# A decoder layer with a mixture of experts: the sample tile in quarters, the first rows block by block, states and most bias rows loaded later

## What is computed

```python
sh1, sc1, g1, sh2, sc2, g2 = split(silu(c) @ w_ada + b_ada, 6)   # per sequence
h = rmsnorm(x, norm1) * (1 + sc1) + sh1
u, gate_b, gate_c, val = split(h @ w_in)                         # 4 x 512 columns
pool_out = (window_mean(u, prefix=state_pool) - u) @ w_pool * pool_scale
conv_out = gate_b * depthwise_conv3(gate_c * val, prefix=state_conv)
x = x + g1 * (concat(pool_out, conv_out) @ w_out)
h2 = rmsnorm(x, norm2) * (1 + sc2) + sh2
logits = h2 @ w_router + b_router                                # top 4 of 32, softmax
y = sum over the 4 of gate * expert(h2)                          # clamped SwiGLU, three 1024x1024
out = rmsnorm(x + g2 * y, final_norm)
```

## Time and profile before

| what | us |
|---|---|
| median of three runs | 1306.57 (1305.33 to 1307.25) |
| the profiled execution's own time | 1306.41 |
| its span, first to last instruction | 1304.6 |
| TensorE busy | 1255.8 (96%) |
| VectorE busy | 525.5 (40%) |
| GpSimd busy | 230.4 (18%) |
| ScalarE busy | 90.9 (7%) |

### The profile page before, as it was taken

The page is one execution under the profiler, slowest core; times in us unless marked ns, Lnnn a source line. Parts: engine busy times, 40 slices in busy tenths (PEclk is TensorE's granted clock), DMA queues, the critical chain, the costliest instruction groups (busy, mean ns, idle before and its releaser), DMA issues.

```text
span 1304.6 us, 32026 instructions
## 1 busy us (share of the span) xinstructions
PE 1255.8 (96%) x14083; PEld 578.7 (44%) x14083; DVE 525.5 (40%) x823; ACT 90.9 (7%) x166; POOL 230.4 (18%) x296
## 2 busy tenths in 40 slices
PE   3999999869999999999999999999999999999997
PEld 2687764523444444333333333333444444433344
DVE  1222313556444444444333333333444444444356
ACT  3210011210000000000000000000000000000002
POOL 5001200030111111122222211121111111112100
PEclk9899999969999999999999999999999999999999
DMA  9877762268999999999999999999999999999994
GB/s 323 278 278 279 274 261 94 104 260 347 408 424 424 426 426 425 425 426 420 421 427 424 423 429 416 425 426 424 425 423 417 427 428 424 427 427 425 423 422 156
DMA packets 63430, 487.32 MB, mean 374 GB/s; under 512 B 11191, under 2 KB 20759, under 8 KB 38053
## 3 DMA queue, kind: packets, MB, share of 16 engines
q1 hardware_dynamic: 47442, 455.92, 84.3%
q0 software_dynamic: 10592, 19.87, 4.2%
q10 hardware_dynamic: 5363, 11.05, 2.3%
HBM read 468.22 MB, written 25.88 MB: 379 GB/s over the span
## 4 chain that ended last, share of the span: by engine, by line
PE 93%; DVE 3%; DMA 2%; issue 1%; ACT 1%; SPq 0%; POOL 0%; DVEq 0%; POOLq 0%
PE acc L1943 51%; PE acc L1968 24%; PE acc L943 9%; PE acc L987 4%; DMA raw<-in_w_ada 2%; PE acc L860 1%; PE acc L2050 1%; PE acc L878 1%; PE acc L998 1%; ACT h_t L486 0%; PE acc L2066 0%; DVE picked L1624 0%; PE acc L959 0%; PE acc L983 0%; POOL rows L1412 0%
## 5 line engine op out<-in xcount | busy, mean ns | idle before, releaser
L1943 PE MATMUL acc<-raw_b,ht 128*32 128x512 f32 x3024 | 332.9, 596 | 5.7 <-DVE ht L1578 5.7
L1943 PE MATMUL acc<-raw,ht 128*32 128x512 f32 x2928 | 319.8, 592 | 0.0
L1681 DVE TENSOR_TENSOR g_sb<-acc,bias_gu 128x768 f32<-128x768 f32 x32 | 30.7, 958 | 521.9 <-PE acc L1943 521.9
L1412 POOL DMA_INDIRECT rows<-h_rows,row_next x90 | 92.7, 1030 | 701.3 <-DVE row_next L1573 654.1
L1943 PEld LDWEIGHTS acc<-raw_b,ht 128*32 128x32 f32 x3024 | 98.3, 111 | 234.7 <-issue 228.2
L1943 PEld LDWEIGHTS acc<-raw,ht 128*32 128x32 f32 x2928 | 95.1, 110 | 205.7 <-issue 200.4
L1968 PE MATMUL acc<-raw,at 128*32 128x256 f32 x2976 | 166.3, 379 | 0.0
L1968 PE MATMUL acc<-raw_b,at 128*32 128x256 f32 x2976 | 166.3, 379 | 0.0
L1968 PEld LDWEIGHTS acc<-raw_b,at 128*32 128x32 f32 x2976 | 96.7, 110 | 77.1 <-issue 18.5
L1968 PEld LDWEIGHTS acc<-raw,at 128*32 128x32 f32 x2976 | 96.7, 110 | 63.9
L943 PE MATMUL acc<-h_t,raw 128*128 128x288 f32 (+1 forms) x512 | 120.1, 397 | 1.1 <-DVE h_t L700 1.1
(11 more groups left out here) (257 smaller groups left out, 646.4 us busy)
## 6 DMA issues: line engine op xcount, KB each, us to landing
raw<-in_w_down SPq DMA_DIRECT2D x33, 2048.0 KB, 12.0
raw<-in_w_gate SPq DMA_DIRECT2D x31, 2048.0 KB, 9.1
raw<-in_w_up SPq DMA_DIRECT2D x31, 2048.0 KB, 13.4
raw_b<-in_w_gate SPq DMA_DIRECT2D x31, 2048.0 KB, 9.8
raw_b<-in_w_up SPq DMA_DIRECT2D x31, 2048.0 KB
raw_b<-in_w_down SPq DMA_DIRECT2D x31, 2048.0 KB
raw<-in_w_ada SPq DMA_DIRECT2D x24, 1024.0 KB, 11.7
expert_rows<-zeros ACTq DMA_DIRECT2D x1, 8704.0 KB, 30.6
```

Source lines behind the costliest of these rows:

```text
L1412: pool.indirect_dma_start(rows[:, b, :], None, h2_quarter, bass.IndirectOffsetOnAxis(ap=idx[:, b:b + 1], axis=0), bounds_check=Q * NTOK - ...
L1681: dve.tensor_tensor(g_sb[:, :, :], gate_of(i, 0), plus(0), ALU.add).then_inc(g_read, 1)
L1943: mm = pe.matmul(gu_of(i)[b][q * TB:(q + 1) * TB, :].rearrange("p (m n) -> p m n", m=2), ht_of(i)[:, b, k, :], w[:, kk, :, q * CW:(q + 1) ...
```

## The change

Five things are edited.

1. **Loads.** Of the bias rows only SH1 and SC1 are loaded at the start (`ada_bias`); G1 to G2, the parameters and the states are issued on ScalarE's queue after its half of the modulation, and four loads of the sample rows in quarters (`x_q`) follow. G1's addition waits for the later biases.
2. **State transposes** move from ahead of SH1's last chunk to between project(2) and project(3); their copies on ScalarE (`empty_states`) stand behind leave(3), ahead of the issue of the clearing transfer and leave(4).
3. **Sample tile.** It is added, scaled and shifted as 128 partitions x 256 columns (`x_q`, `h_q`, `g1_q`, `a2_q`). Its sum of squares is joined over the quarters by a product with `same_s`, made by GpSimd. Its rows are stored in four transfers issued by ScalarE; GpSimd spreads each part's sample rows in four transfers instead of one. ScalarE copies the rows back into `x_sb` for the end.
4. **New states.** "so0" goes from ahead of mix(4) to behind transposes h3; the sample's from behind router(3) to behind the routing matmuls.
5. **First expert.** The three gathers count on semaphores of their own; VectorE turns each block when it has landed, and TensorE does the first half of the contraction block by block (`gate_up_first`), then the second half as before. The sums of the gates on VectorE move behind these transposes.

```diff
@@ ScalarE, front
-            for q in range(Q):
-                lo_, hi_ = q * CPAD, q * CPAD + NC
-                act.dma_start(mod[lo_:hi_, :].rearrange("p (a n) -> p a n", n=QW),
...
+            def ada_bias(a, b, loaded):
...
+            ada_bias(SH1, SC1 + 1, rows_loaded)
             act.wait_ge(tp_full, TP["c"] + 1)
             act.activation(c_sg[:, :, :], c_ps, ACT.Sigmoid).then_inc(tp_free, 1)
             norm_row(n1_rows, norm1, rows_loaded)
-            act.dma_start(par_rows[0:GR, :], pool_scale[0].rearrange("(g p) -> g p", p=P)).then_inc(state_loaded, 16)
-            act.dma_start(par_rows[GR:4 * GR, :], w_conv[0].rearrange("w (g p) -> (w g) p", p=P)).then_inc(state_loaded, 16)
-            act.dma_start(sp_rows, state_pool[0].rearrange("b r d -> (b r) d")).then_inc(state_loaded, 16)
-            act.dma_start(sc_rows, state_conv[0].rearrange("b r d -> (b r) d")).then_inc(state_loaded, 16)
...
                                bias=cols[:, 1, k % 2, k // 2, 0:1]).then_inc(h_mod_a, 1)
+            act.dma_start(par_rows[0:GR, :], pool_scale[0].rearrange("(g p) -> g p", p=P)).then_inc(state_loaded, 16)
+            act.dma_start(par_rows[GR:4 * GR, :], w_conv[0].rearrange("w (g p) -> (w g) p", p=P)).then_inc(state_loaded, 16)
+            act.dma_start(sp_rows, state_pool[0].rearrange("b r d -> (b r) d")).then_inc(state_loaded, 16)
+            act.dma_start(sc_rows, state_conv[0].rearrange("b r d -> (b r) d")).then_inc(state_loaded, 16)
+            ada_bias(G1, PARTS, n2_loaded)
+            for q in range(Q):
+                act.dma_start(x_q[q * NS:(q + 1) * NS, :],
+                              x_sample.rearrange("b t d -> (b t) d")[:, q * QW:(q + 1) * QW]).then_inc(xq_loaded, 16)
...
             for g in range(GR):
                 leave(g, uext[:, g, PAST:PAST + SEQ], uext_s[:, g, :, PAST:PAST + DEC_T])
+                if g == GR - 1:
+                    empty_states()
@@ ScalarE, tail
+            act.wait_ge(x1_ready, TT)
+            act.activation(junk[:, 0:QW], x_q[:, :], ACT.Square, accum_out=ss_q[:, 0:1]).then_inc(act_step, 1)
+            turned(f"h{PT - 1}", PT - 1)
+            act.wait_ge(ss_summed, 1)
+            act.activation(rstd_q[:, :], ss_ps, ACT.Sqrt, bias=eps_c[:, 0:1], scale=1.0 / D).then_inc(sq_done, 1)
+            store(PT - 1)
+            empty(f"h{PT}", h_t[:, :, SEQ:NTOK].rearrange("p (q h) s -> p h q s", q=Q),
+                  tp[:, 0, 0:QW].rearrange("p (h q s) -> p h q s", h=KT // Q, q=Q))
+            act.wait_ge(h_ready, TT + PT + 1)
+            for q in range(Q):
+                act.dma_start(h2_dram[SEQ:NTOK, q * QW:(q + 1) * QW], h_q[q * NS:(q + 1) * NS, :])\
+                    .then_inc(h2_stored[PT % 2], 16)
@@ VectorE, tail
+            dve.wait_ge(mix_done, TT)
+            dve.wait_ge(xq_loaded, 16 * Q)
+            step(dve.tensor_tensor(h_q[:, :], mixp[PT % 2][:, 0, 0:QW], g1_q[:, :], ALU.mult))
+            dve.tensor_tensor(x_q[:, :], x_q[:, :], h_q[:, :], ALU.add).then_inc(x1_ready, 1)
+            dve.wait_ge(x1_ready, TT)
+            step(dve.tensor_tensor(h_q[:, :], x_q[:, :], a2_q[0][:, :], ALU.mult))
+            best(PT - 2)
+            dve.wait_ge(sq_done, TT + 1)
@@ TensorE
-            for k in range(4):
+            for k in range(3):
                 project(k)
+            pe.wait_ge(state_loaded, 16 * 4)
+            take("par")
...
+            project(3)
@@ TensorE, tail
+            pe.matmul(ss_ps, same_s[:, :], ss_q[:, 0:1], start=True, stop=True).then_inc(ss_summed, 1)
+            router(3)
+            take("h4")
+            pe.wait_ge(h_ready, TT + PT + 1)
+            for half in range(KT // Q):
+                mm = pe.transpose(tp[:, 0, half * P:(half + 1) * P], h_q[:, half * P:(half + 1) * P], ident[:, :])
@@ VectorE, first expert
+                def turn_first():
+                    for b in range(SB):
+                        dve.wait_ge(first_gathered[b], 16)
+                        ins = dve.transpose(ht[:, b, :, :], rows[:, b, :].rearrange("p (i k) -> p k i", k=KT))
+                        ins.then_inc(first_turned, 1)
@@ TensorE, first expert
+                def gate_up_first():
...
+                    for b in range(SB):
+                        pe.wait_ge(first_turned, b + 1)
+                        for k in range(KT // 2):
...
+                    mm.then_inc(mm_done, MCH)
+                    gate_up(0, MCH // 2)
...
+                pe.wait_ge(so_ready, 4)
```

More of the change, by code:

```diff
@@ L402, in _ @@
                                         pattern=[[-1, DEC_B], [0, DEC_T]], channel_multiplier=1))
+            step(pool.memset(same_s[:, :], 0.0))
+            for m in range(Q):
+                v = same_s[:, :].rearrange("p (q s) -> p q s", q=Q)
+                step(pool.affine_select(out=v, in_=v, compare_op=ALU.not_equal, fill=1.0, base=-NS * m,
+                                        pattern=[[0, Q], [-1, NS]], channel_multiplier=1))
             step(pool.memset(sel_4[:, :], 1.0))
@@ L621, in _ @@
                     act.wait_ge(rstd_ready, 1)
-                act.activation(ss[0:r, t:t + 1], ss[0:r, t:t + 1], ACT.Sqrt, bias=eps_c[0:r, 0:1],
+                act.activation(ss[:, t:t + 1], ss[:, t:t + 1], ACT.Sqrt, bias=eps_c[:, 0:1],
                                scale=1.0 / D).then_inc(sq_done, 1)
[L624 to L640, removed]
+                if t < PT - 1:
+                    turned(f"h{t}", t)
@@ new lines, in _ @@
+            act.wait_ge(h_ready, TT + PT + 1)
+            for q in range(Q):
+                act.dma_start(h2_dram[SEQ:NTOK, q * QW:(q + 1) * QW], h_q[q * NS:(q + 1) * NS, :])\
+                    .then_inc(h2_stored[PT % 2], 16)
+            act.wait_ge(so0_full, 1)
+            states(0, acc_u)
+            for q in range(Q):
+                act.activation(x_sb[0:NS, PT, q * QW:(q + 1) * QW], x_q[q * NS:(q + 1) * NS, :], ACT.Copy)\
+                    .then_inc(xs_rows, 1)
+            act.wait_ge(so_full, 1)
@@ L642, in _ @@
+            states(2, tp)
+            act.wait_ge(so_ready, 4)
+            for i in range(DEC_T):
+                act.dma_start(new_pool_sample[0, :, PAST - DEC_T + i, :], gate_b[i:NS:DEC_T, 2, 0:DP])\
+                    .then_inc(state_sent, 16)
+            act.dma_start(new_conv_sample[0].rearrange("b r d -> (b r) d"), state_o[3]).then_inc(state_sent, 16)
         @block.vector
@@ L945, in project @@
                     mm.then_inc(z_done, 1)
-            for k in range(4):
+            for k in range(3):
                 project(k)
+            pe.wait_ge(state_loaded, 16 * 4)
+            take("par")
+            pe.transpose(tp[:, 0, 0:4 * GR], par_rows[:, :], ident[0:4 * GR, 0:4 * GR]).then_inc(tp_full, 1)
+            take("st")
+            for g in range(GR):
+                n = DEC_B * PAST
+                pe.transpose(tp[:, 0, g * n:(g + 1) * n], sp_rows[:, g * P:(g + 1) * P], ident[0:n, 0:n])
+            for g in range(GR):
+                n = DEC_B * CPAST
+                mm = pe.transpose(tp[:, 1, g * n:(g + 1) * n], sc_rows[:, g * P:(g + 1) * P], ident[0:n, 0:n])
+            mm.then_inc(tp_full, 1)
+            project(3)
             ada(G1)
@@ L1053, in _ @@
             mm.then_inc(rank_done, 1)
+            pe.wait_ge(new_packed, 4)
+            for g in range(GR):
+                pe.transpose(tp[0:NS, 0, g * P:(g + 1) * P], u_new[:, g, :], ident[:, :])
+            for g in range(GR):
+                mm = pe.transpose(tp[0:DEC_B * CPAST, 1, g * P:(g + 1) * P], v_new[:, g, :], ident[:, :])
+            mm.then_inc(so_full, 1)
         part.close()
@@ L1162, in hybrid_step @@
             row_gathered = sem("row_gathered")
+            first_gathered = [sem(f"first_gathered{b}") for b in range(SB)]
+            first_turned = sem("first_turned")
             g2_spread = sem("g2_spread")
```

169 lines of the change are left out of this document (84 added, 85 removed).

## The result

| | before | after |
|---|---|---|
| median of the runs, us | 1306.86 | 1311.51 |
| lowest and highest, us | 1304.03 to 1307.34 | 1309.99 to 1313.42 |
| profiled execution: time, span, us | 1306.41, 1304.6 | 1309.99, 1308.2 |

The change made the kernel slower: the ratio of the times is 1.0041, with a 95% interval of 1.0028 to 1.0054. That is 5.3 us above the forecast and half a microsecond above its range. The profiled execution of the changed kernel was the shortest of its six, so of these 5.3 us only the 4.0 between the forecast difference of -0.4 and the measured one of +3.6 can be followed in a trace. Medians here are over all executions; two of e2's (1449 and 1858 us) and one of e6's (2253 us) were far longer than the rest, and the ratios leave them out.

The account below looks back on a forecast made before the run. TensorE was taken to bound the kernel from 305.09 us to the end, so only earlier stretches could move: -6.2 (c) + 0.4 (a and b1) + 3.7 (b2) + 1.7 (b3) = -0.4, giving 1306.2 us, range 1304.0 to 1309.0.

Parts of the forecast that it names:

- (b3): Projection: TensorE's clock falls once more than before behind the longer waits, a loss of 1.7 us.
- (b1): Projection's third slice: twelve DMAs queued ahead of leave(0) delay it 5.75 us; less slack 2.2 and front gain 3.1, +0.4.
- (b2): Between project(2) and project(3): the moved state transposes and ScalarE's copies make TensorE wait, a loss of 3.7 us.
- (c): From router(2) to the first expert: earlier ids, quartered sample tile and block-wise start gain 6.2 us.
- (a): Ahead of the projection: transposes leave the chain and fewer loads compete, a gain of 3.1 us (1.7 to 3.6).
- Rival 2: Projection: ScalarE's queue becomes the bound, issues take 9 us, both waits let the clock fall; 1311.2 us, chance 0.17.
- The early slow stretch: Start of the projection: clock at 0.50 from 39 to 45 us; no gain if it goes.
- rival 1: Tail: stores land within 4.8 us, ids release the gathers, at most one clock fall; 1302.0 or 1303.7 us, chance 0.31.
- Rival 3: First expert: block 0 comes no earlier than the others, only the path ahead of the gathers gains; 1309.8 us, chance 0.10.

Follow-up runs that it names:

- e2: The changed kernel with its front put back as before, the x_q loads staying on ScalarE's queue: 1302.28 us, ratio 0.9963 to before.
- e6: Changed kernel, twelve DMAs behind leave(1), parameter and state copies behind leave(4), SyncE's weight loads of slots 4 and 5 held until rows are stored: 1299.14 us.
- e1: The kernel before with only the moved loads and moved state transposes, without x_q: 1313.23 us, ratio 1.0053.
- e3: The changed kernel with ScalarE's copies of parameters and states behind leave(4) in place of leave(3): 1305.82 us, ratio 1.0000 to before.
- e7: The changed kernel with unused matmuls in the two waits of the projection, six and two of them: 1305.30 us, ratio 1.0000 to before.
- e11: The kernel before with x_q and the sample tile in quarters, front and first expert as before: 1305.33 us, ratio 0.9991.
- e10: The changed kernel without the block-wise start, twelve DMAs behind leave(1), parameter and state copies behind leave(4): 1302.06 us, ratio 0.9962 to before.
- e8: The kernel before with only the block-wise start of the first expert: 1305.26 us, ratio 0.9996.
- e9: The kernel before with the block-wise start, VectorE's pair values waiting for GpSimd's issue of expert 1's gathers: 1305.65 us, ratio 0.9992.
- e13: The kernel before with the block-wise start, VectorE's pair values held until expert 1's first gather has landed: 1302.22 us, ratio 0.9975.

## Why the prediction was wrong

By its own steps; where it said -0.4, the profiled executions differ by +3.6, 3.4 of it ahead of 308.46. The steps below miss by +3.6 (b3), +0.7 (b1), +0.1 (b2) and -0.9 (c), 3.5 in all.

- **(a) The front, gain 3.1: right.** The projection started at 38.22 in place of 41.84, 3.6 sooner, the upper bound. Over all traces it is more: 36.3 to 40.2 in the kernels with the new front, 41.3 to 43.2 in those with the old one.
- **(b1) ScalarE's queue, +0.4 net: the mechanism right, the size short.** The twelve issues cost 4.7 us, under the 5.35. But the router bias behind them took 7.83 where I had allowed 4.61 + 0.4. The third slice began at 59.39, 1.1 later than before (about 58.3, counted back from 102.54 by the 44.2 us that 192 such matmuls take), with 6.25 us of idle time. Rival 2 had this as its place. With loads put ahead of it that issue took 6.3 to 9.1 us (e1, e2, e3, e7, e11 and after), without them 2.3 to 6.0. What exactly it waits for no run tells apart; that the queue refuses descriptors, as the prediction has it, is a reading of the long issue that no run shows.
- **(b2) States between the projections, +3.7: right.** It is 3.85.
- **(b3) The clock, +1.7: the step that failed.** Both waits let it fall, 2.15 + 1.47 = 3.6 us, and mix(4) had a fall of 1.7 that before did not have: 5.3 us. I took one fall more than before as the likeliest, and priced it by the short one of 3.4 us, although the waits just computed, 2 to 4 and 2.5 us, were longer than the 1.1 us behind which the clock had fallen. e7 shows that the 3.6 hang on the idle time in the waits: with these filled, the kernel is level with before (ratio 1.0000). The 1.7 of mix(4) may be chance. The early slow stretch was called no gain because ScalarE sets b1; that held.
- **(c) Tail and first expert, gain 6.2: 5.4, or 7.1 without the clock's 1.7 in mix(4), so near, but by other numbers.** The ids came 2.5 sooner after router(2) than before, forecast 3.6. The stores landed 7.7 us behind the last issue, forecast 5.6, so they, not the ids, released the gathers, as the forecast had it and rival 1 did not. TensorE started 4.9 us nearer to gather 0 (9.0 to 4.1), forecast 3.6; the blocks are some 3.0 to 3.7 of it, for with the rows used together e11 and e10 have 7.1 and 7.35, gather 1 there no longer running beside the slot comparison. In the trace of after the chain goes through the second gather of expert 1 (289.51, 4.76 us), but TensorE waits only 0.53 us behind it. The forecast followed the first expert's own rows and not those of expert 1.
- **The rivals.** Rival 3, that the start in blocks does nothing, is wrong for the changed kernel and right for that part alone (e8), by another mechanism than the one it named: block 0 did come early. Rival 2 gave 1311.2, near the 1311.5 that was measured, with both waits and both falls as it said. But it is right in part by luck: it wanted 3.3 us more wait ahead of the third slice, from 8.4 us of issues on, and the issues and what they pushed back took 4.7 + 3.2 more for the router bias, 7.9. That slice came 0.7 later than forecast, and the falls, longer and more than it had them, did the rest. Rival 1 needed the stores within 4.8 us; the last took 7.7.

## What to carry to other kernels

Before moving work off the start of a kernel, look for the one engine that is never idle behind it, and count for each wait that you put into its run the wait and the slow clock after it: here 1.5 to 3 us for each wait of 2.4 to 6.5 us, and nothing behind the one of 1.65 in e11. A DMA issue is not cheap because the last one was; put a batch of them behind the evacuation that somebody waits for, not ahead of it: moving the same twelve issues gained 9.7 us. And if an early start gains nothing, follow the second chain: the next item's transfer is often what the first item's end really waits for.

## What the hardware showed that I had not expected

- Unused matmuls in two waits made the kernel 5.4 us faster by the ratios (e7), though the third slice began only 0.5 sooner.
- One issue on ScalarE's queue, of a small bias, blocked the engine for 2.3 to 9.1 us, by what was issued before it and what else was under way.
- A wait on GpSimd's own increment let VectorE pass before a gather that stood ahead of it in GpSimd's program had run (e9); a wait on the landing did not.
- A gather issue of GpSimd takes 1.0 us, and beside a long two-input instruction of VectorE it ends 0.9 to 1.0 us behind that instruction's end, wherever in it the gather began: 4.77 us when it began 0.3 behind the start of one of 4.16 (e8), 4.01 when it began 1.0 behind (before), 3.04 and 2.68 beside one of 2.16 (e6, before). e13 undid it.
